# Norm seams of a two-block transformer kernel: feature sums, first product tiles and the place of the norm's scale

## The chip, the cores and the metric

One core of a Trainium2 chip runs the whole program. The metric is the device time of one execution in microseconds; the median of a few executions is compared. The engines are called PE (TensorE), DVE (VectorE), ACT (ScalarE), POOL (GpSimd) and SP (SyncE, which issues the weight loads).

## The reference

256 tokens with D = 1024 features go through a first block of two layers (beside a context of 256 tokens, which is needed until the last mixer) and a second block of two layers. Everything is float32. Cut to what matters:

```
# first block, layer l; x and the context xc alike
h  = x * (1 + scale1) + shift1
y  = mixers(h @ w_in)          # GLA, MLA, convolution module, gated and merged, @ w_out
x  = layer_norm(a * x + gate1 * y)                    # ln1
x  = layer_norm(a * x + gate2 * conv_ffn(x * (1 + scale2) + shift2))   # ln2
# inside the convolution module: silu(layer_norm(conv(h))) @ conv_wo

# second block, layer i
y  = attention(rms_norm(h, g_mix_pre[i]) @ w_in)      # stick-breaking, then dilated
h  = h + rms_norm(y @ w_out, g_mix_post[i])
f  = square(relu(rms_norm(h, g_ffn_pre[i]) @ w_ff_in[i])) @ w_ff_out[i]
h  = h + rms_norm(f, g_ffn_post[i])
h  = h + (p[i] @ w_ple[i]) * sigmoid(rms_norm(h, g_ple[i]) @ w_ple_gate[i])
```

Both norms run over the 1024 features of a token; the layer norm needs mean and mean square, the rms norm the mean square alone. At this point the context matters only in this: layer 0 works on 512 columns (256 tokens and 256 of context), layer 1 after its mixers and the second block on 256.

## The kernel before

The activations lie feature-major in SBUF: X is 8 feature tiles (KD = 8) of 128 partitions with a column for each token. So a norm's sum over features runs across partitions, and the kernel takes it on PE: `sums` (L904 to L910) multiplies each of the 8 feature tiles by a constant matrix of ones and adds the eight products in one PSUM tile, which then holds the sum in every partition. A layer norm needs two such tiles (`resid_sum`: X, and `resid_sq`: the squares that ACT makes), an rms norm one.

Weights come in 1 MB chunks into a ring of three (SP issues them, chunk n when chunk n-3 has been used). Every engine's program is written out by hand, block by block, and the class `Plan` (from L140) only fixes which PSUM bank (of 8) each tile gets, and the order of tiles and chunks; the engines' programs must follow that order.

Three forms of product stand at the seams.

- `cols` (L773): float32, one tile of 128 output features after another, for each tile 8 matmuls over k, the feature tile of the operand. The profile shows two records for each such matmul.
- `parts` (L743): layer 0's FFN `up` product. Operand and weights are split in a high half (fp32r) and a low half, and a tile takes three matmuls for each k. ACT makes the high half of the weights, POOL the low half (L726), two buffers of each.
- `narrow_cols` (L818, with `thrice` L811 to L816): the same three products in the second block, 256 columns. ACT makes the high half of a weight tile, `narrow_hi` (L1418), DVE the low half, `narrow_lo` (L2393); `narrow(u)` runs three tiles ahead of tile u, with four buffers.

A layer norm goes like this. ACT takes a product's tile out of PSUM with the gate as its scale (L1480), DVE adds it to X (`residual`, L2016), ACT squares X. When all tiles are done PE takes both sums. DVE forms mean and variance (`moments`, L1982 to L1992, from L1986), ACT the square root, DVE the reciprocal (L1973), then for each feature tile DVE subtracts the mean and multiplies (L2022, L2023), ACT applies gain and offset (`scaled`, L1488), and DVE modulates it by scale and shift (`operand_a`: L1941, or L1950 where the operand is split, with L1962 for the low half, and ACT the high half between). The first product tile runs through k as the operand arrives, and the second tile after it.

In the second block `post` (L2410) normalises a mixer's or the FFN's output and adds it to X (L2415, L2417); ACT squares X; PE sums; `rms` and `root` give 1/rms in the tile RS; `pre` (L2395) forms the operand X * g * RS on DVE (L2400), ACT rounds it to the high half, and DVE takes the low half (L2405). The FFN's relu is L2556 and its square L2558 with the split L2544; the gate of the last part (ple) is a sigmoid on ACT, with L2580 to L2582 on DVE.

The convolution runs on DVE. Its norm (`cln`) is summed on PE straight after the product cq, and DVE normalises right behind, before the two latent rms norms of MLA (L2295 to L2299). ACT's convolution sigmoids and DVE's products (L2305, L2306) come after the gate tiles co.0, and then ACT takes the tiles of the uq product (PE L1164) out of PSUM as mla_qn and mla_qr.

## Time and profile before

| | before |
|---|---|
| median of 3 runs | 3613.69 us (3610.08 to 3616.46) |
| profiled execution, its own time | 3616.7 us |
| its span | 3614.6 us |
| mean granted PE clock | .949 |
| PE busy | 3214.1 us, 89% of the span |
| DVE busy | 1715.0 us, 47% |
| ACT busy | 1024.0 us, 28% |
| POOL busy | 150.9 us, 4% |
| ACT_TABLE_LOAD at L1378 | 120 times |

How to read it: an engine's share is an average over stages with different limits, so PE's 89% doesn't say where the other 11% lie. The waits list for each engine what ended its idle time. A timeline row gives start and length in us (x16 means that sixteen instructions of a kind stand in it), and in brackets the idle time of the engine just before with what ended it. An operation whose line is that of a helper is told by its tile: L1378 is ACT's helper, so there the name behind it counts. The granted clock is a share of full speed, 1.00 for 2.4 GHz and .50 for 1.2 GHz.

### The profile page before, as it was taken

How to read it: one execution, taken by the hardware profiler on the slowest of the kernel's cores; microseconds unless marked ns; L12 is line 12 of the kernel's file. 1: busy time of each engine (PE TensorE's matmuls, PEld its weight loads, DVE VectorE, ACT ScalarE, POOL GpSimd, SP SyncE). 2: the span in 40 equal slices, each digit the busy share in tenths (PEclk: the TensorE clock that was granted, in tenths of full speed). 3: DMA queues.
4: the chain of work that ended last, by engine and by line, in shares of the span. 5: the costliest groups of instructions: out<-in, count | busy, mean ns of one | idle time of the engine just before them, and what ended most of it. 6: DMA issues, size and time to landing. Idle time of an engine off the chain costs nothing.

```text
span 3614.6 us, 38987 instructions
## 1 busy us (share of the span) xinstructions
PE 3214.1 (89%) x15931; PEld 2335.8 (65%) x15931; DVE 1715.0 (47%) x2857; ACT 1024.0 (28%) x1645; POOL 150.9 (4%) x125
## 2 busy tenths in 40 slices
PE   6978798999999789998988899989978898977898
PEld 3655454444444378743777666878877888975887
DVE  2268876241211268702367932235154655734555
ACT  3132210122230233202332033221145434423333
POOL 4000000000000044300000000000000000000000
PEclk9989799999999999998998999999999999978999
DMA  5221124322233222222221332334542454411552
GB/s 187 82 59 35 47 91 138 121 61 83 104 100 121 70 82 94 79 80 63 77 64 59 111 100 79 115 123 148 155 143 71 140 154 138 140 41 56 152 157 89
DMA packets 419440, 362.26 MB, mean 100 GB/s; under 512 B 20848, under 2 KB 392612, under 8 KB 419264
## 3 DMA queue, kind: packets, MB, share of 16 engines
q1 hardware_dynamic: 416928, 359.11, 31.6%
q8 instruction: 127, 2.08, 0.2%
q0 software_dynamic: 2336, 0.67, 0.1%
q14 instruction: 49, 0.40, 0.0%
HBM read 358.70 MB, written 1.05 MB: 100 GB/s over the span
## 4 chain that ended last, share of the span: by engine, by line
PE 73%; DVE 17%; issue 4%; ACT 4%; DMA 1%; POOL 1%; DVEq 0%; ACTq 0%; POOLq 0%
PE banks L783 13%; PE banks L893 13%; PE banks L758 7%; PE banks L875 6%; DVE conv_out L2145 5%; PE banks L814 4%; PE banks L815 4%; PE banks L816 4%; PE banks L805 3%; PE banks L909 3%; PE banks L1137 2%; ACT narrow_hi L1378 2%; PE banks L916 1%; PE banks L1128 1%; DVE gla_att L2207 1%
## 5 line engine op out<-in xcount | busy, mean ns | idle before, releaser
L2393 DVE TENSOR_TENSOR narrow_lo<-wring,narrow_hi 128x1024 fp32r<-128x1024 f32 x204 | 248.0, 1224 | 266.4 <-ACT narrow_hi L1378 265.8
L783 PE MATMUL banks<-operand_a,wring 128*128 128x256 f32 (+1 forms) x1184 | 345.4, 455 | 29.1 <-DVE operand_a L1941 29.1
L814 PE MATMUL banks<-operand_narrow,narrow_hi 128*128 128x256 f32 x960 | 289.4, 301 | 41.1 <-DVE operand_narrow L2405 24.3
L783 PEld LDWEIGHTS banks<-operand_a,wring 128*128 128x128 f32 x1184 | 228.8, 194 | 145.5 <-issue 121.3
L2145 DVE SCALAR_TENSOR_TENSOR conv_out<-conv_in,vectors,conv_out 128x512 f32<-128x512 f32 (+1 forms) x464 | 286.7, 618 | 15.2
L893 PE MATMUL banks<-operand_a,wring 128*128 128x512 f32 (+1 forms) x768 | 264.0, 499 | 22.7 <-DMA wring<-in_w_in_dram 13.6
L815 PE MATMUL banks<-operand_narrow,narrow_hi 128*128 128x256 f32 x960 | 276.4, 288 | 0.0
L816 PE MATMUL banks<-operand_narrow,narrow_lo 128*128 128x256 f32 x960 | 276.2, 288 | 0.0
L893 PEld LDWEIGHTS banks<-operand_a,wring 128*128 128x128 f32 x768 | 146.0, 194 | 132.9 <-issue 98.1
L1378 ACT ACTIVATE narrow_hi<-wring 128x1024 fp32r<-128x1024 f32 x204 | 212.0, 1049 | 67.6 <-PE banks L816 66.2
L875 PE MATMUL banks<-ffn_h,wring 128*128 128x512 f32 (+1 forms) x704 | 227.4, 486 | 0.0
L814 PEld LDWEIGHTS banks<-operand_narrow,narrow_hi 128*128 128x128 f32 x960 | 187.9, 196 | 55.6 <-issue 23.5
L1128 PE MATMUL banks<-operand_a,wring 128*128 128x512 f32 (+1 forms) x512 | 183.3, 515 | 19.3 <-DVE conv_in L2163 19.3
L875 PEld LDWEIGHTS banks<-ffn_h,wring 128*128 128x128 f32 x704 | 133.8, 190 | 92.9 <-issue 83.5
L815 PEld LDWEIGHTS banks<-operand_narrow,narrow_hi 128*128 128x128 f32 x960 | 189.4, 197 | 0.6
L893 PE MATMUL banks<-operand_b,wring 128*128 128x512 f32 (+1 forms) x512 | 174.5, 498 | 17.2 <-DMA wring<-in_mla_wo_dram 6.3
L816 PEld LDWEIGHTS banks<-operand_narrow,narrow_lo 128*128 128x128 f32 x960 | 189.0, 197 | 0.0
L726 POOL TENSOR_TENSOR weights_lo<-wring,weights_hi 128x1024 fp32r<-128x1024 f32 x44 | 108.9, 2476 | 1360.3 <-ACT weights_hi L1378 1360.3
L758 PE MATMUL banks<-operand_a_hi,weights_hi 128*128 128x512 f32 x352 | 138.0, 392 | 29.9 <-POOL weights_lo L726 29.9
L814 PE MATMUL banks<-ff_h,narrow_hi 128*128 128x256 f32 x512 | 149.1, 291 | 16.5 <-DVE ff_h L2544 11.2
L1128 PEld LDWEIGHTS banks<-operand_a,wring 128*128 128x128 f32 x512 | 102.6, 206 | 84.7 <-issue 76.8
L1378 ACT ACT_TABLE_LOAD x120 | 154.0, 1283 | 2.8 <-PEq L2603 0.7
(326 smaller groups left out, 5454.0 us busy)
## 6 DMA issues: line engine op xcount, KB each, us to landing
wring<-in_w_in_dram SPq DMA_DIRECT2D x52, 1024.0 KB, 5.1
wring<-in_w_ada_dram SPq DMA_DIRECT2D x48, 1024.0 KB, 6.4
wring<-in_ffn_wup_dram SPq DMA_DIRECT2D x44, 1024.0 KB, 5.0
wring<-in_w_ff_in_dram SPq DMA_DIRECT2D x32, 1024.0 KB, 5.4
wring<-in_w_ff_out_dram SPq DMA_DIRECT2D x32, 1024.0 KB, 5.7
wring<-in_ffn_wdown_dram SPq DMA_DIRECT2D x32, 704.0 KB, 4.6
wring<-in_w_in_dram SPq DMA_DIRECT2D x36, 512.0 KB, 5.0
wring<-in_w_in_dil_dram SPq DMA_DIRECT2D x18, 1024.0 KB, 4.9
```

Of the source, the lines that this page charges most:

```text
L726: pool.tensor_tensor(WL[:, u % 2, :, :], w, WH[:, u % 2, :, :].bitcast(F32), ALU.subtract).then_inc(ev("w_lo"), 1)
L758: mm = pe.matmul(bank(t, 0, n), w[:, k, :], x[:, k, 0:n], start=first, stop=last)
L783: mm = pe.matmul(bank(t, 0, n), w[:, k, j * P:(j + 1) * P], opnd[:, k, 0:n], start=k == 0, stop=k == kt - 1)
L814: pe.matmul(out, wh, a[:, 0:SEQ], start=first, stop=False)
L815: pe.matmul(out, wh, a[:, SEQ:512], start=False, stop=False)
L816: return pe.matmul(out, wl, a[:, 0:SEQ], start=False, stop=last)
L875: mm = pe.matmul(bank(t, 0, n), w[:, k % per, :], opnd[:, k, 0:n], start=k == 0, stop=k == kt - 1)
L893: mm = pe.matmul(bank(t + j, 0, n), w[:, k, j * P:(j + 1) * P], (AF if gate else opnd)[:, k, 0:n], start=k == 0, stop=k == KD - 1)
L1128: mm = pe.matmul(bank(t, 0, n), w[:, k, :], AF[:, k, 0:n], start=k == 0, stop=k == KD - 1)
L1378: act.activation(dst, src, f, **kw).then_inc(*inc)
L2145: own(stt(dst, src, w, dst, ALU.mult, ALU.add))
L2393: tt(NL[:, v % 4, :, :], w, NH[:, v % 4, :, :].bitcast(F32), ALU.subtract).then_inc(ev("narrow_lo"), 1)
```

## The change

It has five parts.

1. **Sums by DVE.** For ln1, ln2 and the convolution norm DVE keeps running totals over the eight feature tiles (X in `TD[0]`, the squares in `TD[1]`) while the product before still runs, seven adds each, and PE multiplies just the two totals by the ones.
2. **The layer norm's loop.** The first two centrings stand ahead of the wait for the square root. ACT does gain and offset and the modulation tile by tile, and the high half where there is one, DVE only the low half.
3. **First tiles together.** Of the next product the first tiles are taken together over k: the gate tile (in layer 1 with two key tiles), two tiles of `up` in layer 0 and four in layer 1, three tiles in the second block. For that, two weight splits move into the residual loop before, and the next weights are split one tile earlier (`more=4`); the first four low halves of the second block are POOL's.
4. **The second block's 1/rms at the exit from PSUM.** The operand is X * g alone. The squares' ones-matmuls stand between the product's matmuls. RS is applied by DVE at the eviction (Q and K of layer 0, relu, gate), through the cos and sin tables (layer 1), or as a scale for each token (V, for which PE turns RS in the tile `rc`). Bank 7 is kept for such small tiles.
5. **The convolution norm** moves behind co.0's gates and the latent norms.

The diff, cut to its core. On PE:

```diff
+        def moments(t, n, at=0):
+            for i in range(2):
+                start_tile(t + i)
+                counter("ln_sum", 1)(0)
+                pe.matmul(bank(t + i, 0, n), cn("ones"), TD[:, at + i, 0:n], start=True,
+                          stop=True).then_inc(*made(t + i))
...
-            cols_a(f"gr{l}", 512, a_ready())
+            first_tiles(512, a_ready(), (f"gr{l}", 1), *([(f"k{l}", 2)] if l else []))
...
             cols_a(f"cq{l}", n)
-            sums(F[f"cln{l}"], CV, 0, KD, n, lambda m: pe.wait_ge(ev("conv_out"), KD * l + m + 1))
-            sums(F[f"cln{l}"] + 1, SQC, 0, KD, n, lambda m: pe.wait_ge(ev("conv_sq"), KD * l + m + 1))
...
+            run(branch(f"co{l}", CV, n, None, (0,)))
             t = F[f"krr{l}"]
...
-            run(branch(f"co{l}", CV, n, None, (0,)))
+            moments(F[f"cln{l}"], n, 2)
...
-            for i, (name, src) in enumerate((("resid_sum", X), ("resid_sq", SQB))):
-                sums(F[f"ln1_{l}"] + i, src, 0, KD, n, counter(name, KD))
-            cols_a(f"up{l}", n, a_ready())
+            moments(F[f"ln1_{l}"], n)
+            first_tiles(n, a_ready(), (f"up{l}", 4 if l else 2))
+            cols_a(f"up{l}", n, 4 if l else 2)
...
+        def first_tiles(n, ready, *names):
+            for k in range(KD):
+                ready(k)
+                for t, pairs in tiles:
+                    for j, (w, x) in enumerate(pairs):
+                        mm = pe.matmul(bank(t, 0, n), w[:, k, :], x[:, k, 0:n], start=k + j == 0,
+                                       stop=k == KD - 1 and j == len(pairs) - 1)
+                    if k == KD - 1:
+                        mm.then_inc(*made(t))
...
+            for k in range(KD if ready else 0):
+                ready(k)
+                for i in range(together):
+                    mm = thrice(bank(t0 + i, 0, SEQ), v0 + i, k, AN[:, k, :], k == 0, k == KD - 1)
+                    if k == KD - 1:
+                        mm.then_inc(*made(t0 + i))
+                add(k - 1)
```

On ACT (DVE's `narrow` changes alike; the root that moves is the convolution norm's):

```diff
-        def narrow(u, more=3):
+        def narrow(u, more=4):
...
+        def high(g, m):
+            op(AN[:, m, 0:SEQ], X[:, m, 0:SEQ], ACT.Copy, (ev("n_hi"), 1), scale=vec(g, m))
+        def deviation2(x, t):
+            act.wait_ge(*done(t))
+            op(x, bank(t, 0, SEQ), ACT.Sqrt, free(t), scale=1.0 / D, bias=EPSC)
...
+        def operand_split(m):
+            modulated(TD[:, m % 2, :], 0, 3, m, 2).then_inc(ev("a_full"), 1)
+            act.wait_ge(ev("a_full"), m + 1)
+            op(AH[:, m, :], TD[:, m % 2, :], ACT.Copy, (ev("a_hi"), 1))
...
-            root(TD[:, 3, 0:n])
             for m in range(3, 5):
                 latent(m)
+            co = gates(f"co{l}", l, 2 * KD, n)
             root(TD[:, 0, 0:n])
             root(TD[:, 0, :])
-            co = gates(f"co{l}", l, 2 * KD, n)
             next(co)
             next(co)
+            root(TD[:, 3, 0:n])
```

On POOL, behind `down0`, and on DVE:

```diff
+        for v in range(4):
+            _, w = narrow_weights(v)
+            pool.wait_ge(ev("narrow_hi"), v + 1)
+            pool.tensor_tensor(NL[:, v, :, :], w, NH[:, v, :, :].bitcast(F32), ALU.subtract).then_inc(ev("narrow_lo"), 1)
...
+        def scale(t):
+            n_scale[0] += 1
+            dve.wait_ge(*freed(t))
+            dve.reciprocal(RS, RS).then_inc(ev("scale"), 1)
+            dve.wait_ge(ev("scale"), n_scale[0])
+
+        def post(t, name, g, g2):
+            dve.wait_ge(*freed(t))
+            own(dve.reciprocal(RSP, RSP))
+            for m in range(KD + 1):
+                if m < KD:
+                    dve.wait_ge(*freed(F[name] + m))
+                    own(stt(TD[:, m % 2, 0:SEQ], Y[:, m, :], vec(g, m), RSP, ALU.mult, ALU.mult))
+                    resid2[0] += 1
+                    tt(X[:, m, 0:SEQ], X[:, m, 0:SEQ], TD[:, m % 2, 0:SEQ], ALU.add).then_inc(ev("resid2"), 1)
+                    dve.wait_ge(ev("resid2"), resid2[0])
+                if m:
+                    operand2(g2, m - 1)
...
-                    ts(x, bank(t, 0, SEQ), 0.0, None, ALU.max).then_inc(*free(t))
+                    if m == 0 and h == 0:
+                        scale(F[f"fpre{l}"])
+                    stt(x, bank(t, 0, SEQ), 0.0, RS, ALU.max, ALU.mult).then_inc(*free(t))
```

How the instructions move, at three places. First ACT around layer 0's convolution norm (conv_sq are the squares of the convolution's output, the one tmp_dve row behind them the norm's square root, the two-fold one the latents' roots; tmp_act from banks are co.0's gates, tmp_act from conv_out the convolution's sigmoids). Before:

```order
L1378 ACTIVATE conv_sq<-conv_out 128x512 x8
L1378 ACT_TABLE_LOAD
L1378 ACTIVATE tmp_dve<-tmp_dve 128x512
L1660 ACTIVATE latents<-banks,vectors 128x512
L1378 ACTIVATE latent_squares<-banks,vectors 128x512
L1660 ACTIVATE latents<-banks,vectors 128x512
L1378 ACTIVATE latent_squares<-banks,vectors 128x512
L1378 ACTIVATE tmp_dve<-tmp_dve 128x512 x2
L1378 ACT_TABLE_LOAD
L1378 ACTIVATE tmp_act<-banks,vectors 128x512 x2
L1378 ACTIVATE tmp_act<-conv_out,vectors 128x512 x8
L1378 ACTIVATE mla_qn<-banks 128x512 x2
```

and with the change:

```order
L1473 ACT_TABLE_LOAD
L1473 ACTIVATE tmp_dve<-tmp_dve 128x512 x2
L1473 ACT_TABLE_LOAD
L1473 ACTIVATE tmp_act<-banks,vectors 128x512 x2
L1473 ACT_TABLE_LOAD
L1473 ACTIVATE tmp_dve<-tmp_dve 128x512
L1473 ACT_TABLE_LOAD
L1473 ACTIVATE tmp_act<-conv_out,vectors 128x512 x8
L1473 ACTIVATE mla_qn<-banks 128x512 x2
```

The norm's root went from ahead of the last two latents to behind the gates, with two more table loads.

Second, ACT from the last residual tile before the first FFN on. Before (operand_a_hi is the operand's high half, weights_hi the weights'):

```order
L1480 ACTIVATE tmp_act<-banks,mod 128x256 x2
L1378 ACTIVATE squares_b<-resid 128x512 x2
L1378 ACT_TABLE_LOAD
L1378 ACTIVATE tmp_dve<-tmp_dve 128x512
L1378 ACTIVATE resid<-resid,vectors 128x512 x8
L1378 ACTIVATE operand_a_hi<-tmp_dve 128x512 x8
L1378 ACTIVATE weights_hi<-wring 128x1024 x2
```

and with the change:

```order
L1473 ACTIVATE weights_hi<-wring 128x1024
L1607 ACTIVATE tmp_act<-banks,mod 128x256 x2
L1473 ACTIVATE squares_b<-resid 128x512 x2
L1473 ACT_TABLE_LOAD
L1473 ACTIVATE tmp_dve<-tmp_dve 128x512
L1473 ACTIVATE resid<-resid,vectors 128x512
L1558 ACTIVATE tmp_dve<-resid,mod 128x256 x2
L1473 ACTIVATE operand_a_hi<-tmp_dve 128x512
```

The weights' high halves stand ahead of the norm now, and scaling, modulation and high half follow one another for each feature tile.

Third, PE at the seam into the second block. Before:

```order
L875 MATMUL banks<-ffn_h,wring 128x256 x176
L909 MATMUL banks<-resid,consts 128x256 x8
L909 MATMUL banks<-squares_g,consts 128x256 x8
L909 MATMUL banks<-b_sq,consts 128x256 x8
L814 MATMUL banks<-operand_narrow,narrow_hi 128x256
L815 MATMUL banks<-operand_narrow,narrow_hi 128x256
L816 MATMUL banks<-operand_narrow,narrow_lo 128x256
```

and with the change, up to the second feature tile's square (L876):

```order
L864 MATMUL banks<-operand_narrow,narrow_lo 128x256
L862 MATMUL banks<-operand_narrow,narrow_hi 128x256
L863 MATMUL banks<-operand_narrow,narrow_hi 128x256
L864 MATMUL banks<-operand_narrow,narrow_lo 128x256
L876 MATMUL banks<-b_sq,consts 128x256
L862 MATMUL banks<-operand_narrow,narrow_hi 128x256
```

The 24 ones-matmuls ahead of the product are gone; two stand in their place (`L998 MATMUL banks<-tmp_dve,consts 128x256 x2`), and the rms norm's eight stand between the product's nine-fold steps.

## Rows read from the trace of the kernel before

**Rows 1.** The page: shares of the chain that ended last, and three groups by line

```profile
PE 73%; DVE 17%; issue 4%; ACT 4%; DMA 1%; POOL 1%; DVEq 0%; ACTq 0%; POOLq 0%
...
L2393 DVE TENSOR_TENSOR narrow_lo<-wring,narrow_hi 128x1024 fp32r<-128x1024 f32 x204 | 248.0, 1224 | 266.4 <-ACT narrow_hi L1378 265.8
...
L1378 ACT ACTIVATE narrow_hi<-wring 128x1024 fp32r<-128x1024 f32 x204 | 212.0, 1049 | 67.6 <-PE banks L816 66.2
...
L1378 ACT ACT_TABLE_LOAD x120 | 154.0, 1283 | 2.8 <-PEq L2603 0.7
```

**Rows 2.** Waits of PE: line, releaser: us in total, times, longest us

```profile
PE banks L909 <- ACT b_sq L1378: 35.4, 16, 13.5
...
PE banks L758 <- POOL weights_lo L726: 29.9, 1, 29.9
PE banks L783 <- DVE operand_a L1941: 29.1, 3, 16.8
```

**Rows 3.** Timeline, norm before the first FFN: start, us, engine, line, [idle before <- releaser]

```profile
1231.58 7.03 PE L909 MATMUL banks<-resid,consts 128*128 128x512 f32 x16
...
1232.65 0.69 DVE L2016 SCALAR_TENSOR_TENSOR resid<-resid,tmp_act 128x512 f32<-128x512 f32 x1 [6.17 <-ACT tmp_act L1480]
...
1247.43 3.35 DVE L1973 RECIPROCAL tmp_dve<-tmp_dve 128x512 f32<-128x512 f32 x1 [0.70 <-ACT tmp_dve L1378]
...
1252.27 0.81 ACT L1378 ACTIVATE resid<-resid,vectors 128x512 f32<-128x512 f32 x1 [4.87 <-DVE resid L2023]
...
1275.37 0.79 PE L758 MATMUL banks<-operand_a_hi,weights_hi 128*128 128x512 f32 x1 [29.90 <-POOL weights_lo L726]
```

**Rows 4.** Timeline of PE at the norm into layer 1 and layer 1's first norm

```profile
1668.13 7.03 PE L909 MATMUL banks<-resid,consts 128*128 128x512 f32 x16
...
1698.87 9.29 PE L783 MATMUL banks<-operand_a,wring 128*128 128x512 f32 x16 [16.85 <-DVE operand_a L1941]
...
2367.13 3.62 PE L909 MATMUL banks<-resid,consts 128*128 128x256 f32 x16
...
2384.62 8.62 PE L783 MATMUL banks<-operand_a,wring 128*128 128x256 f32 x28 [10.42 <-DVE operand_a L1941]
```

**Rows 5.** Windows: stretch, us, busy PE PEld DVE ACT POOL, granted clock, DMA share, GB/s

```profile
1699.00:1703.00 4.00, 4.00 (x5) 1.69 (x6) 4.00 (x14) 0.00 (x0) 0.00 (x0) 0.50 0.00 0
...
2649.00:2651.00 2.00, 1.56 (x10) 0.95 (x8) 1.68 (x5) 1.43 (x3) 0.00 (x0) 1.00 0.00 0
```

**Rows 6.** Timeline at the first uq tiles of layer 0

```profile
777.46 1.06 ACT L1378 ACTIVATE mla_qn<-banks 128x512 f32<-128x512 f32 x2
...
778.18 6.23 PE L1164 MATMUL banks<-operand_b,wring 128*128 128x512 f32 x10 [2.56 <-ACT mla_qn L1378]
```

**Rows 7.** Timeline of the second block's norms in layer 0

```profile
2614.96 3.62 PE L909 MATMUL banks<-resid,consts 128*128 128x256 f32 x16
...
2657.39 0.38 ACT L1378 ACTIVATE b_qk<-banks 128x256 f32<-128x256 f32 x1 [1.55 <-PE banks L816]
...
2783.48 3.62 PE L909 MATMUL banks<-b_sq,consts 128*128 128x256 f32 x16
...
2812.26 0.42 DVE L2556 TENSOR_SCALAR tmp_dve<-banks 128x256 f32<-128x256 f32 x1
...
3015.55 3.62 PE L909 MATMUL banks<-b_sq,consts 128*128 128x256 f32 x16
...
3023.21 0.42 ACT L1378 ACTIVATE b_sq<-resid 128x256 f32<-128x256 f32 x1 [2.80 <-DVE resid L2417]
...
3068.11 0.39 ACT L1378 ACTIVATE tmp_act<-banks 128x256 f32<-128x256 f32 x1 [1.54 <-PE banks L816]
```

**Rows 8.** Timeline of DVE and POOL in the first FFN

```profile
1304.85 0.75 DVE L2370 SCALAR_TENSOR_TENSOR tmp_dve<-ffn_up,vectors,tmp_dve 128x512 f32<-128x512 f32 x1
...
1306.73 2.40 POOL L726 TENSOR_TENSOR weights_lo<-wring,weights_hi 128x1024 fp32r<-128x1024 f32 x1 [3.04 <-ACT weights_hi L1378]
...
1306.88 2.79 DVE L2370 SCALAR_TENSOR_TENSOR tmp_dve<-ffn_up,vectors,tmp_dve 128x512 f32<-128x512 f32 x1
```

More of the change, by code:

```diff
@@ L175, in tiles, with gemm @@
             self.place(self.first[name] + j)
-    def gemm(self, name, chunks, split=lambda i: False, after=lambda: None):
-        self.reserve(name, sum(ends for _, ends in chunks))
-        self.chunk0[name], t = len(self.chunk_at), self.first[name]
+    def gemm(self, name, chunks, split=lambda i: False, after=lambda: None, done=0, total=0):
+        if not done:
+            self.reserve(name, total or sum(ends for _, ends in chunks))
+            self.chunk0[name] = len(self.chunk_at)
+        t = self.first[name] + done
         for i, (loads, ends) in enumerate(chunks):
@@ L831, in narrow_rows, with row_scale @@
+        def row_scale(l):
+            t = F[f"rc{l}"]
+            start_tile(t)
+            pe.wait_ge(ev("scale"), 3 * l + 1)
+            for tok in range(2):
+                mm = pe.matmul(bank(t, tok, tok + 1), RS[:, tok * P:(tok + 1) * P], cn("ident")[:, 0:1], start=True,
+                               stop=True)
+            mm.then_inc(*made(t))
         def narrow_rows(name):
@@ L1755, in _ @@
             ffn_sigmoid(FT1 - 1)
[L1756 to L1757 removed]
+            if l == 0:
+                residual(f"down{l}", l, 5, n, SQG, pl.last(f"wout{l}"))
+                scaled(l, "l2g", "l2b", n, operand(2, 1, 0, 2))
         resid2 = [0]
[L1761 to L1773 removed]
+        act.wait_ge(ev("eps_set"), 1)
@@ L2080, in _, with keys @@
                ALU.add).then_inc(*free(t))
+            def keys(m0, m1):
+                for m in range(m0, m1):
+                    t = F[f"k{l}"] + m
+                    dve.wait_ge(*done(t))
+                    ts(K[:, m, :], bank(t), vec(f"bk{l}", m), None, ALU.add).then_inc(*free(t))
+            keys(0, 2 * l)
             for m in range(8):
@@ L2105, in _ @@
             dve.wait_ge(*freed(F[f"z{l}"] + 7))
-            for m in range(4):
-                t = F[f"k{l}"] + m
-                dve.wait_ge(*done(t))
-                ts(K[:, m, :], bank(t), vec(f"bk{l}", m), None, ALU.add).then_inc(*free(t))
+            keys(2 * l, 4)
             for m in range(4):
@@ L2583, in _ @@
                 dve.wait_ge(ev("resid2"), resid2[0])
+            for m in range(KD):
+                t = F[f"pg{l}"] + m
+                narrow(pl.narrow_first[f"pg{l}"] + m)
+                dve.wait_ge(*done(t))
+                if m == 0:
+                    scale(F[f"ple{l}"])
+                tt(TA[:, m % 2, 0:SEQ], bank(t, 0, SEQ), RS, ALU.mult).then_inc(*free(t))
+                if m:
+                    add_row(m - 1)
+            add_row(KD - 1)
     core.close()
```

520 lines of the change are left out of this document (299 added, 221 removed).

## The prediction

> **What bounds the kernel now.** The time after an average over stages says little, so I read the views in this order. The page first: the chain that ended last is 73% TensorE (PE) and 17% VectorE (DVE) [rows 1]. So only two things can pay: PE work taken away, or PE waits closed. Next the waits of PE [rows 2]: three groups belong to norms, 35.4 us before ones-matmuls that wait for squares, 29.9 us before one L758 tile, and 29.1 us in three waits for a modulated operand. Then the timeline around each of those places [rows 3, 4, 6, 7], and the windows for the granted clock [rows 5]. In them the reader is to see that at each norm three costs stand behind one another: the feature sums on PE, a chain of small DVE and ScalarE (ACT) steps with PE idle, and a first product tile that must end before its evictor starts. The engines that take over the work, DVE and ACT, are idle there.
>
> I sum each seam from the last product before it to the point where the next steady stage is reached. Gains have a plus.
>
> **Layer norm before the first FFN (ln1, layer 0): +16.5.** Before, the first sums start at 1231.58 (7.03 us, and as much again for the squares), the reciprocal at 1247.43 (3.35 us), ACT's first scaling at 1252.27, and PE's first product at 1275.37, after 29.90 idle [rows 3]. A float32 matmul of 512 columns takes .86 (7.03 for eight); one of the three products takes a quarter, so a tile of 24 some 5.3, and two are done at 1288.8 with 2.8 for a slow start. After: the last totals end about 1235.5 (the residual row's successor: an eviction, one add into X and three adds at .7), two single matmuls .9, the variance, root and reciprocal chain (as in rows 3, 9.0 from the first sum's end less the 5.5 that DVE waited for the second, and 1.4 of centring hidden under the root), so the first normed tile stands at 1243.6. From there ACT feeds: scale .81 [rows 3], modulation in two halves, between 2 x .42 [rows 7] and 2 x .60, I take 1.0, high half .63, together 2.5 per feature tile: eight end at 1264. PE needs 1.4 per feature tile and follows: 1266. The next tile waits for its weight split, 1.05 [rows 1] on ACT and 2.40 on POOL [rows 8] behind an eviction: 1270 to 1272. That is 16.5 to 18.5 saved; I take the low end. If ACT's modulation took 1.2, 1.6 less.
>
> **Layer norm into layer 1 (ln2, layer 0): +16.5.** Before, sums at 1668.13, first product at 1698.87, and its 16 matmuls take 9.29 instead of 6.9 [rows 4], because PE's granted clock is .50 (1.2 of 2.4 GHz) for the first 4 us after the idle time [rows 5]. The 8 gate tiles follow, then the keys at 6.9 a tile. After: first operand 14 us after the sums' place, 1682, gate tile and two key tiles together, 6 matmuls of .43 per feature tile, 20.6, plus 2.2 for the low clock: 1704.9. Before, the same three tiles end at 1708.2 + 13.7. Saved 1721.9 - 1704.9 = 17; .5 off for the split key loop.
>
> **ln1, layer 1: +9.** Sums at 2367.13, product at 2384.62, four tiles until 2400.9 [rows 4]. After: first operand at 2375.9 (the reciprocal is 1.75 for 256 columns), four tiles of .43 make 1.73 per feature tile, 8 x 1.73 + 2.2 low clock: 2391.9.
>
> **Into the second block (ln2 of layer 1, first rms): +16.5.** Sums at 2614.96; PE idles 13.5 us before the squares' sums [rows 2]; the third tile's eviction is at 2657.39 [rows 7]. After: normed from 2622.2, three tiles together with one square matmul per feature tile, PE 1.51 (nine products at .12, a quarter of 3.62 / 8, and one square at .43), ACT 1.55 (scale, high, square). Four weight low halves now run on POOL, 2.40 each. The row at 1306.88 shows a DVE instruction of .75 becoming 2.79 while POOL's runs [rows 8]. That adds between 0 and 8 us; I take 3, because ACT and not DVE is the slowest feeder. Tiles at about 2640.
> By the Trainium skill, "GPSIMD Engine Reference", Key points, POOL shares its SBUF interfaces with VectorE, and DVE instructions with two SBUF inputs contend for them, which speaks against this part of the change. By that rule, with which the trace agrees, all four stand in the DVE chain, 4 x 2.0, and leave +11.5 here instead of +16.5.
>
> **The other rms seams.** Post and pre norm of layer 0's FFN: 2783.48 to the first relu at 2812.26 [rows 7]. After, six squares add 2.6 to the product, the sums (3.6) and the second norm's sums and root (about 8) leave, but the post loop gets a third DVE step (.42 to .48 for 128x256, as the ACT row at 3023.21 [rows 7], and some .05 between two): 1.48 x 8 from 2790.5, then PE's last column, root, reciprocal and four weight halves that are now taken one earlier: relu at 2809. **+3.2**. The one-earlier split also delays the second half's first relu by a high and a low half, 1.05 + 1.22 [rows 1], twice in all: **-4.3**. Layer 1's output product is half as long, too short for four weight splits ahead of it, so its seam gives nothing: **-.2**. FFN post norm and gate: 3015.55 to the last gate tile's eviction at 3068.11 [rows 7]; after, the product ends at 3018.1 with its squares, the root, the reciprocal and the pw evictions take 11.5, eight steps of 1.48 follow, three tiles are done at 3041.7, and five at 3.2 (high and low half, eviction) and the eviction follow: 3059.3, **+8.6**, and the same in layer 1, **+8.6**. Second mixer's pre norm: no norm chain ahead of 24 tiles, **+5**. Last add through one more DVE step: **-.5**. Scales of V rows, cos and sin tables and Q/K on DVE run beside PE: nothing, as ACT and DVE have idle time in those products; if that cover went, 16 x .42 = 6.7 us.
>
> **The convolution norm: -3.7 and -5.7.** This is the part where I go against the change. The sums leave PE (2 x 7.03, less two matmuls: 12 us), but PE is not what ends this stage: ACT evicts the uq tiles only after eight convolution sigmoids, and PE already waits 2.56 for that at 778.18 [rows 6]. The norm is now placed behind the gates and the latent norms, and ACT gets two more table loads per layer, 1.28 each [rows 1]. I place the last sigmoid at about 780, against 777 before, so the third tile starts 3 us later, PE idles some 17 us before, and .7 of low clock is added. Layer 1 is the same with no slack: 3.5 later and 2.2 of low clock. Bounds: if PE led, +12 and +5.2.
>
> Queues: SP's ring order is that of the plan, where only the keys' chunks stand around the gate tiles; each load is issued three chunks ahead, so nothing there is late.
>
> **The sum.** 16.5 + 16.5 + 9 + 16.5 + 3.2 - 4.3 - .2 + 8.6 + 8.6 + 5 - .5 - 3.7 - 5.7 = 69.5. The profiled execution took 3616.7; its span was 3614.6. 3616.7 - 69.5 = 3547.2. The median of the runs shown is 3.0 lower, so I forecast 3545 as the median.
>
> **Rivals.**
> - *PE led at the convolution norm* (.10). For: PE has 12 us less to do. Against: the 2.56 wait for ACT. +17 instead of -9.4: 3518.
> - *The fed phases stay slow for part of their time* (.13). PE is fed in drops, ACT-bound, and its clock had risen to 1.00 by 2649 in such a phase [rows 5]. If it falls again between drops, some 30 us are lost: 3575.
> - *The second block gives nothing* (.09). DVE's third step per tile, POOL against DVE, and earlier splits eat +3.2, +8.6 and +5: 3570.
> - *Slower: low clock throughout.* At full clock the matmuls of the phases taken together are 10.9 + 20.6 + 13.8 + 6 x 12.1 = 118 us. At .50 they take twice as long. From 70 us of these at half clock on, the gain is gone; all of it gives about 3650. For: the first 4 us at .50 after idle [rows 5]. Against: the window at 2649, 1.00 with PE busy 1.56 of 2.00 [rows 5]. (.03)
> - *The change doesn't do what it says* (.02). The totals on DVE could be on the path themselves: 14 adds of .7 per norm, if DVE were late in the product. DVE's wait of 6.17 for ACT before such a step speaks against it [rows 3]. Then each norm gives 5 less: 3570.
>
> **Chances.** My forecast .62; the two cases at 3570 and 3575 and the one at 3518 are taken in by the range: my own terms' bounds give 3530 to 3561, and the range is 3518 to 3577. A measurement of this kernel tells .2%, 7.2 us, from no change. Every case but the slow clock lies far below 3606; I give faster .95, same .01, slower .04, with some left for a wait that I don't see.
>
> **What would show it.** After: in the waits of PE no ones-matmul row above 5 us; L758's first wait near 11 us instead of 29.9; the modulated operand's longest near 9 instead of 16.8; each next product's first matmul starting while the norm's loop still runs on DVE; uq's third tile still waiting for ACT's mla_qn, about 3 us later after the convolution; four POOL rows near 2.4 just before the second block, with longer DVE rows beside them; clock .50 only in the first 4 to 5 us of each such phase. The prediction is wrong if the uq tiles start earlier with PE never waiting for mla_qn, if the clock stays at .50 through a whole fed phase, or if the three rms seams of a layer give under 5 us together.

## The result, and the profile after

The changed kernel takes 3583.44 us (median of 4 executions, 3580.98 to 3585.38) against 3615.07 for the kernel before: the ratio is .9912, with a 95% interval of .9895 to .9929, or 32 us faster. The forecast was 3545, the range began to be wrong above 3577, and of the forecast gain of 69.5 us less than half came. Its profiled execution has a span of 3581.4 us, 33.2 less than before.

The page of the changed kernel, the same lines as [rows 1]:

```profile
PE 70%; DVE 16%; ACT 6%; issue 6%; DMA 1%; POOL 1%; DVEq 0%; ACTq 0%; POOLq 0%
...
L1473 ACT ACTIVATE narrow_hi<-wring 128x1024 fp32r<-128x1024 f32 x204 | 213.0, 1051 | 161.6 <-PE banks L864 151.9
...
L1473 ACT ACT_TABLE_LOAD x124 | 159.1, 1283 | 2.9 <-PEq L2795 0.7
```

PE's busy time fell by 55 us (3214.1 to 3159.1), so PE did give up the work; but the span fell by 33 only, and its share of the last chain went from 73 to 70%, ACT's from 4 to 6. The waits of PE say what took its place, in the columns of [rows 2]:

```profile
PE banks L862 <- DVE operand_narrow L2561: 36.2, 7, 13.9
...
PE banks L1260 <- ACT mla_qn L1473: 29.8, 2, 17.6
PE banks L862 <- DVE tmp_dve L2736: 26.0, 34, 2.1
...
PE banks L862 <- DVE ff_h L2722: 23.1, 12, 3.2
...
PE banks L811 <- DVE operand_a_lo L2073: 14.4, 6, 10.2
PE banks L811 <- ACT operand_a L1558: 14.2, 2, 8.9
...
PE banks L876 <- ACT b_sq L1473: 8.7, 13, 2.7
```

The waits of [rows 2] are shorter (35.4 before ones-matmuls is 8.7, 29.9 is 10.2 for the longest, 29.1 is 14.2). In their place stand 29.8 us for ACT's mla_qn behind the convolution (4.5 before), which the prediction had foreseen, and 26.0 + 23.1 us for DVE in the FFN of the second block: L2736 is the relu, which frees PE's banks (no such wait before), and ff_h the operand of the second product (11.2 us before). That second pair it had not foreseen. The ones-matmuls still have two rows above the 5 us that the prediction allowed: the 8.7 here, and 9.1 at L998, four waits of at most 2.5.

To see where the time went, I took the same event in both traces at the end of each seam (before, after), and compared how far the changed kernel is ahead there.

| up to | before | after | gained here | forecast |
|---|---|---|---|---|
| convolution norm, layer 0: first mla_qn | 777.46 | 780.39 | -2.9 | -3.7 |
| ln1, layer 0: third FFN tile's eviction | 1294.22 | 1277.46 | 15.4, and 4.3 ahead of it | 16.5 |
| ln2, layer 0: keys and what follows | 2073.47 | 2041.15 | 15.6 | 16.5 |
| convolution norm, layer 1: fourth mla_qn | 2140.25 | 2113.62 | -5.7 | -5.7 |
| ln1, layer 1: second table load behind the first tiles | 2401.45 | 2365.80 | 9.0 | 9 |
| into the second block: last Q/K tile | 2694.83 | 2647.94 | 11.2 | 16.5 |
| FFN, layer 0: first relu | 2812.26 | 2763.25 | 2.1 | 3.2 |
| second half's first relu | 2916.14 | 2869.86 | -2.7 | -2.15 |
| post norm and gate: last gate tile | 3068.11 | 3033.84 | -12.0 | +8.6 |
| second mixer: last Q/K tile | 3159.88 | 3124.32 | 1.3 | 5 |
| FFN, layer 1: first relu | 3347.43 | 3313.31 | -1.4 | -.2 |
| second half's first relu | 3451.41 | 3419.69 | -2.4 | -2.15 |
| post norm and gate, layer 1 | 3606.91 | 3572.76 | 2.4 | 8.6 |

The 4.3 us in the second row lie between the convolution norm and the output product ahead of ln1, and no term of the forecast stands for them: 2.8 of them are PE's waits for three weight loads, which fell from 11.2 to 8.4. They are not the norm's: with the norm put back, the stretch from the first mla_qn to that product takes 396.0 us, in the changed kernel 394.8, before 399.1.

How far one execution can be trusted here can be read from the nine traces (this one, the control and seven of the experiments) whose program is the same up to this point. The first mla_qn comes anywhere from 777.7 to 784.7 in them, so the first row's -2.9 means little as a place. But counted from the first latent ahead of it, it comes after 79.04 or 79.05 us in all nine, against 76.05 before: 3.0 lost, and .9 more for the low clock behind PE's idle time. The seam of ln1 gives 15.2 to 17.3 us in the nine.

So the first five rows are right to about a microsecond each. What is missing is in the second block: 5 us at its entry, 20.6 and 6.2 at the two gates, 3.7 at the second mixer, 2 to 3 at the FFNs' starts. The three seams of a layer there (mixer or entry, FFN's start, gate) give 1.3 us together in layer 0 and 2.3 in layer 1; under 5 was the prediction's own sign of being wrong.

The first block's first norm, in the columns of [rows 3]:

```profile
1232.94 3.37 PE L998 MATMUL banks<-tmp_dve,consts 128*128 128x512 f32 x4 [2.54 <-DVE tmp_dve L2151]
...
1238.93 3.35 DVE L2081 RECIPROCAL tmp_dve<-tmp_dve 128x512 f32<-128x512 f32 x1
...
1243.05 0.81 ACT L1473 ACTIVATE resid<-resid,vectors 128x512 f32<-128x512 f32 x1 [4.81 <-DVE resid L2174]
...
1246.52 0.77 PE L811 MATMUL banks<-operand_a_hi,weights_hi 128*128 128x512 f32 x1 [10.21 <-DVE operand_a_lo L2073]
...
1253.92 0.50 PE L811 MATMUL banks<-operand_a_hi,weights_hi 128*128 128x512 f32 x1 [0.85 <-DVE operand_a_lo L2073]
```

The sums take PE 3 us instead of 14, the first product starts at 1246.5 instead of 1275.4, and then PE gets a feature tile every 2.5 us (each with about .85 idle): the forecast chain, step by step.

The clock is not as forecast everywhere. Two stretches of this seam and two at the entry to the second block, in the columns of [rows 5]:

```profile
1250.70:1267.60 16.90, 10.67 (x39) 6.53 (x38) 9.98 (x17) 14.73 (x24) 1.02 (x1) 1.00 0.00 1
1267.80:1274.40 6.60, 5.21 (x12) 4.13 (x13) 1.88 (x1) 0.14 (x1) 4.12 (x2) 0.50 0.18 52
2591.10:2598.80 7.70, 6.58 (x27) 6.11 (x28) 6.52 (x15) 7.54 (x17) 2.38 (x1) 0.50 0.72 246
2599.00:2607.00 8.00, 8.00 (x60) 7.70 (x59) 1.10 (x3) 1.97 (x5) 0.00 (x0) 1.00 0.01 2
```

Behind the phase that ACT feeds, in which PE was busy for 10.67 of 16.90 us, the granted clock fell to .50 once more, and at the second block's entry it stayed at .50 for the first 7.9 us of PE's work, not 4.

And the loop that holds the second block, DVE and then ACT in the first product of layer 0's FFN:

```profile
2780.72 1.23 DVE L2555 TENSOR_TENSOR narrow_lo<-wring,narrow_hi 128x1024 fp32r<-128x1024 f32 x1 [1.43 <-ACT narrow_hi L1473]
2781.86 0.42 DVE L2722 TENSOR_TENSOR ff_h<-tmp_dve,ff_h 128x256 fp32r<-128x256 f32 x1
2782.20 0.42 DVE L2736 SCALAR_TENSOR_TENSOR tmp_dve<-banks,gate_rank 128x256 f32<-128x256 f32 x1
2782.65 0.42 DVE L2738 TENSOR_TENSOR tmp_dve<-tmp_dve 128x256 f32<-128x256 f32 x1
2784.51 1.23 DVE L2555 TENSOR_TENSOR narrow_lo<-wring,narrow_hi 128x1024 fp32r<-128x1024 f32 x1 [1.43 <-ACT narrow_hi L1473]
```

```profile
2783.11 0.42 ACT L1473 ACTIVATE ff_h<-tmp_dve 128x256 fp32r<-128x256 f32 x1 [2.42 <-DVE tmp_dve L2738]
2783.43 1.04 ACT L1473 ACTIVATE narrow_hi<-wring 128x1024 fp32r<-128x1024 f32 x1
```

Read them as one chain: weight's low half, operand's low half, relu, square on DVE; copy and next high half on ACT; next low half on DVE. It closes every 3.79 us, while the 24 matmuls of a tile take 2.88, and neither engine is idle for a reason of its own. The relu period is 3.79 in both kernels, in all four half products. Two relus of the kernel before:

```profile
2819.84 0.42 DVE L2556 TENSOR_SCALAR tmp_dve<-banks 128x256 f32<-128x256 f32 x1
...
2823.62 0.42 DVE L2556 TENSOR_SCALAR tmp_dve<-banks 128x256 f32<-128x256 f32 x1
```

The gate's loop is another case. Before, ACT alone evicted its tiles and waited for PE (the 1.54 in the last row of [rows 7]), one tile every 2.88 us. In the changed kernel DVE scales the tile first, behind the weight's low half, and two of ACT's sigmoids stand 3.37 us apart:

```profile
3020.37 0.42 ACT L1473 ACTIVATE tmp_act<-tmp_act 128x256 f32<-128x256 f32 x1 [1.70 <-DVE tmp_act L2772]
...
3023.74 0.42 ACT L1473 ACTIVATE tmp_act<-tmp_act 128x256 f32<-128x256 f32 x1 [1.70 <-DVE tmp_act L2772]
```

This chain was made by the change. In layer 1, where no further weights have to be split, the last sigmoids stand 1.2 to 1.3 us apart.

### The profile page after: what moved, and what is told of

Same layout as the page of the kernel before. It is cut to its first block, busy times and chain, and to the rows that moved or that the text cites. A ratio compares the mean times of both kernels' runs of the same rounds, so it can differ in the third digit from the quotient of the medians.

```text
span 3581.4 us, 38780 instructions
## 1 busy us (share of the span) xinstructions
PE 3159.1 (88%) x15771; PEld 2306.4 (64%) x15771; DVE 1734.6 (48%) x2863; ACT 1049.8 (29%) x1685; POOL 160.7 (4%) x130
## 3 DMA queue, kind: packets, MB, share of 16 engines
HBM read 358.70 MB, written 1.05 MB: 100 GB/s over the span
## 4 chain that ended last, share of the span: by engine, by line
PE 70%; DVE 16%; ACT 6%; issue 6%; DMA 1%; POOL 1%; DVEq 0%; ACTq 0%; POOLq 0%
PE banks L982 13%; PE banks L830 12%; PE banks L779 6%; PE banks L964 6%; DVE conv_out L2306 4%; PE banks L853 3%; PE banks L862 3%; PE banks L864 3%; PE banks L863 3%; ACT narrow_hi L1473 3%; PE banks L1234 2%; PE banks L1013 2%; PE banks L1225 1%; PE banks L811 1%; DVE gla_att L2368 1%
## 5 line engine op out<-in xcount | busy, mean ns | idle before, releaser
L830 PE MATMUL banks<-operand_a,wring 128*128 128x256 f32 (+1 forms) x1056 | 298.8, 446 | 0.0
L2306 DVE SCALAR_TENSOR_TENSOR conv_out<-conv_in,vectors,conv_out 128x512 f32<-128x512 f32 (+1 forms) x464 | 286.8, 618 | 15.2
L830 PEld LDWEIGHTS banks<-operand_a,wring 128*128 128x128 f32 x1056 | 202.3, 192 | 97.2 <-issue 77.7
L982 PEld LDWEIGHTS banks<-operand_a,wring 128*128 128x128 f32 x768 | 147.2, 195 | 133.2 <-issue 98.7
L982 PE MATMUL banks<-operand_b,wring 128*128 128x512 f32 (+1 forms) x512 | 173.1, 495 | 15.2 <-DMA wring<-in_gla_wo_dram 6.7
L862 PE MATMUL banks<-ff_h,narrow_hi 128*128 128x256 f32 x512 | 152.9, 299 | 26.0 <-DVE ff_h L2722 23.1
L1225 PEld LDWEIGHTS banks<-operand_a,wring 128*128 128x128 f32 x512 | 101.4, 204 | 85.0 <-issue 77.5
L982 PEld LDWEIGHTS banks<-operand_b,wring 128*128 128x128 f32 x512 | 97.0, 193 | 82.0 <-issue 63.7
```

Of the source, the lines that this page charges most:

```text
L830: mm = pe.matmul(bank(t, 0, n), w[:, k, j * P:(j + 1) * P], opnd[:, k, 0:n], start=k == 0, stop=k == kt - 1)
L862: pe.matmul(out, wh, a[:, 0:SEQ], start=first, stop=False)
L982: mm = pe.matmul(bank(t + j, 0, n), w[:, k, j * P:(j + 1) * P], (AF if gate else opnd)[:, k, 0:n], start=k == 0, stop=k == KD - 1)
L1225: mm = pe.matmul(bank(t, 0, n), w[:, k, :], AF[:, k, 0:n], start=k == 0, stop=k == KD - 1)
L2306: own(stt(dst, src, w, dst, ALU.mult, ALU.add))
```

## The experiments

Each run is the changed kernel with one edit, unless it says otherwise; times are medians, ratios are to the kernel before on the same chip, with their 95% intervals.

**The changed kernel again.**

> The changed kernel once more, as the foot that the other runs are read against. Both theories: its ratio to before stays near .991, a time near 3583 us, and its trace shows the same stages as before: relu to relu 3.79 us in the FFN's first product, uq's third tile waiting some 17 us for ACT in layer 0.

Measured: 3580.32, ratio .9912 (.9897 to .9926). The medians of the changed kernel were 3583 and 3580, so below, differences of under 4 us are told only where a trace shows them. "Less" is against the control.

**The convolution norm put back.** Ones-matmuls, norm and root stand where they stood.

```diff
+            sums(F[f"cln{l}"], CV, 0, KD, n, lambda m: pe.wait_ge(ev("conv_out"), KD * l + m + 1))
+            sums(F[f"cln{l}"] + 1, SQC, 0, KD, n, lambda m: pe.wait_ge(ev("conv_sq"), KD * l + m + 1))
             cols_a(f"ckv{l}", 512)
...
-            moments(F[f"cln{l}"], n, 2)
```

> The convolution norm as it was before the change (ones-matmuls over all feature tiles behind cq, norm ahead of the latents), all else as changed. My theory, that this part of the change costs time: the sigmoids come earlier again, uq's third tile starts about 3 and 3 us sooner and the low clock behind PE's idle time goes, so 9 to 10 us less than the changed kernel, near 3574. Rival, that PE leads there and the sums were the cost: 12 us more for each layer, near 3600.

Measured: 3572.42, ratio .9891 (.9875 to .9908), 8 us less than the control. The intervals overlap, but the rival's 3600 is far off, and the trace has the two parts: from the first latent to the first mla_qn 75.6 us instead of 79.0, and in layer 1 from the sixth merged tile to the fourth mla_qn 67.3 instead of 72 to 74.

**The convolution norm between ckv and kr, totals on DVE kept.**

```diff
             cols_a(f"ckv{l}", 512)
+            moments(F[f"cln{l}"], n, 2)
             cols_a(f"kr{l}", 512)
...
             totals(3, SQC, n, lambda m: dve.wait_ge(ev("conv_sq"), KD * l + m + 1))
+            moments(F[f"cln{l}"], n)
...
```

The loop that normalises moves with it ahead of kr, and ACT's root ahead of the gates.

> The convolution norm's totals on DVE as changed, but the two ones-matmuls and the whole norm between the products ckv and kr instead of behind the gates. My theory, that the place and not the totals costs time: PE is 12 us earlier in layer 0 and 5 in layer 1, and the sigmoids, which need only the gates by then, follow: 20 to 26 us less than the changed kernel, near 3560. Rival, that PE now waits for DVE's totals behind the convolution: no better than with the norm put back, near 3574.

Measured: 3559.65, ratio .9851 (.9837 to .9866), 21 us less than the control. In its trace PE waits for no mla_qn at the place of [rows 6]; ACT reaches it 11 us earlier than in the changed kernel (780.39), and PE's 6.26 idle are for an operand of its own:

```profile
761.38 13.96 PE L1262 MATMUL banks<-operand_b,wring 128*128 128x512 f32 x25 [6.26 <-DVE operand_b L2463]
```

```profile
769.37 1.06 ACT L1475 ACTIVATE mla_qn<-banks 128x512 f32<-128x512 f32 x2
```

So the totals on DVE are worth 13 us (against the run with the norm put back), and the place behind the gates gave all of it back and another 8.

**Eviction ahead of the weight's low half, on DVE** (FFN, gate, and Q and K of layer 0).

```diff
                     x = TD[:, 2 + m % 2, 0:SEQ]
-                    narrow(pl.narrow_first[f"ffin{l}.{h}"] + m)
-                    if m:
-                        low_half(m - 1)
...
                     tt(x, x, x, ALU.mult).then_inc(ev("ff_full"), 1)
+                    if m:
+                        low_half(m - 1)
+                    narrow(pl.narrow_first[f"ffin{l}.{h}"] + m)
```

> On DVE alone, in the second block's products, the eviction of tile u (with the norm's scale and the square) stands ahead of the low half of weight tile u+4 instead of behind it. Theory A, that in these loops DVE and ACT form one chain (low half, eviction, square, ACT's copy, ACT's next high half, next low half: 3.79 us a tile in the FFN, 3.37 in the gate) and that this is where the expected gain was lost: the periods fall to PE's 2.9, that is 64 x .9 = 57 us, 16 x .45 = 7 us, and 1 to 2 us at each of five first tiles: 60 to 70 us less, near 3518. Theory B, that PE or the weight ring sets these periods: less than 10 us less, and the relu period stays above 3.5.

Measured: 3505.3, ratio .9701 (.9687 to .9716), 75 us less than the control, above the 60 to 70 expected. The chain is open, DVE now waits for PE:

```profile
2856.57 1.23 DVE L2555 TENSOR_TENSOR narrow_lo<-wring,narrow_hi 128x1024 fp32r<-128x1024 f32 x1
2858.29 0.42 DVE L2733 SCALAR_TENSOR_TENSOR tmp_dve<-banks,gate_rank 128x256 f32<-128x256 f32 x1 [0.50 <-PE banks L864]
2858.75 0.42 DVE L2735 TENSOR_TENSOR tmp_dve<-tmp_dve 128x256 f32<-128x256 f32 x1
2859.09 0.42 DVE L2722 TENSOR_TENSOR ff_h<-tmp_dve,ff_h 128x256 fp32r<-128x256 f32 x1
2859.45 1.23 DVE L2555 TENSOR_TENSOR narrow_lo<-wring,narrow_hi 128x1024 fp32r<-128x1024 f32 x1
```

2.88 from low half to low half, PE's own pace. Theory B is out.

**Squares two tiles behind.** In the FFN's last product PE's `add(m - 1)` becomes `add(m - 2)`, with the last two behind it.

> The changed kernel, but the ones-matmul of a square in the FFN's last product stands two tiles behind the tile it belongs to, not one. Theory A: PE waits there for ACT's square, some .5 us at each of seven tiles in both layers, so 6 to 8 us less, near 3574. Theory B, that these waits are idle time which the weights' arrival would give anyway: within 2 us of the changed kernel.

Measured: 3571.49, ratio .9879 (.9866 to .9893), 9 us less; the trace has 4.2 and 3.7 us in the two products. In the changed kernel each tile had a wait like this. With the lag they are gone (8.7 us in 13 waits became 2.7 in 2):

```profile
2957.99 0.70 PE L876 MATMUL banks<-b_sq,consts 128*128 128x256 f32 x2 [0.53 <-ACT b_sq L1473]
```

**One first tile alone in the second block.** `together` is 1 instead of 3.

> The changed kernel, but in the second block the first product tile alone is taken while the operand arrives, not three together. Theory A: in the FFN and the gate the loop of DVE and ACT sets the pace behind the first tile, so the two extra tiles that are ready early wait for their eviction and the seams of FFN and gate (four of six) lose nothing; the two seams before Q and K lose 3 to 5 us each: 5 to 10 us more, near 3590. Theory B, that PE's start was the gain: five to six us at each of six seams, 30 us more, near 3612.

Measured: 3569.84, ratio .9872 (.9859 to .9886): 10 us less, where both theories expected more. The three tiles taken together cost time. The windows of the changed kernel at the start of layer 0's FFN, in the columns of [rows 5]:

```profile
2744.50:2748.50 4.00, 3.94 (x18) 3.97 (x19) 3.79 (x10) 2.32 (x7) 0.00 (x0) 0.50 1.05 329
2749.00:2758.00 9.00, 9.00 (x67) 8.70 (x66) 3.97 (x9) 2.45 (x6) 0.00 (x0) 1.00 0.00 1
```

PE is saturated from its first matmul, at .50 for the first 4.5 us, and ends at 2758.8; DVE had fed the last feature tile by 2753.3. With one tile PE follows the feed, and the first relu comes at 2759.55 instead of 2763.25, with the product before it ending at the same time. And as the loop behind it takes 3.79 for each of 16 tiles, in order, two further tiles that lie ready in PSUM are worth nothing. The trace has 3.8 and 3.4 us at the two first relus, counted from the norm's first reciprocal, and 2 at each gate. At the entry the first Q tile comes 4.9 us earlier, and the last Q/K tile no earlier.

**The first low halves on DVE, behind the norm.** POOL's four instructions leave; DVE makes all four at the first Q tile.

> The changed kernel, but the second block's first four low halves are made by DVE as all others, not by POOL. Theory A, that POOL's 2.4 us instructions hold DVE's norm steps up (1.20 for .42, 1.80 for .42, 1.67 for .48 in the changed kernel's trace, and a wait): DVE's own 4 x 1.22 fall in the same stretch, three of them in its idle time before the norm, so 2 to 4 us less. Theory B, that POOL takes work off the path: 3 to 5 us more.

Measured: 3596.93, ratio .9943 (.9929 to .9956), 17 us more. The edit did more than it was meant to: it put the low halves behind the whole norm, and PE needs three before its first matmul:

```profile
2605.51 0.55 PE L858 MATMUL banks<-operand_narrow,narrow_hi 128*128 128x256 f32 x1 [19.73 <-DVE narrow_lo L2549]
```

**The same in DVE's idle time.** Two before the last residual tile, one before the moments, the last behind the norm.

> The changed kernel, with the second block's first low halves on DVE again, but in its idle time: two before the last residual tile, the third before the norm's moments, the fourth behind the norm. The first try had put all four behind the norm, and PE waited 19.73 us for them. Theory A, that POOL holds DVE up: DVE's steps fall back from 1.20, 1.80 and 1.67 to .42 and .48, the third half costs .8, PE waits for no low half: 2 to 3 us less. Theory B, that ACT feeds and DVE's delays don't count: within 1 us in the trace at the first Q tile.

Measured: 3575.27, ratio .9892 (.9878 to .9905). The ratio doesn't part it from the control; the trace does. First the changed kernel's DVE, then this one's:

```profile
2580.08 1.20 DVE L2147 SCALAR_TENSOR_TENSOR resid<-resid,tmp_act 128x256 f32<-128x256 f32 x1 [8.15 <-ACT tmp_act L1607]
...
2583.57 1.80 DVE L2096 TENSOR_TENSOR tmp_dve<-tmp_dve 128x256 f32<-128x256 f32 x1
```

```profile
2579.38 0.42 DVE L2152 SCALAR_TENSOR_TENSOR resid<-resid,tmp_act 128x256 f32<-128x256 f32 x1 [1.31 <-ACT tmp_act L1603]
...
2582.82 0.42 DVE L2092 TENSOR_TENSOR tmp_dve<-tmp_dve 128x256 f32<-128x256 f32 x1
```

From the last residual step to the first Q tile it takes 29.0 us (2579.38 to 2608.42) instead of 32.0 (2580.08 to 2612.06): the 3 us that the prediction had put down for POOL.

**Three tiles ahead.** `narrow(u, more=3)` on both engines.

> The changed kernel with the weights' halves made three tiles ahead as before, not four. Theory A: the first relu of each half no longer stands behind a high and a low half, 1.05 + 1.22 in the second halves (twice) and 1.2 to 2.3 at each first tile of six products: 8 to 12 us less, near 3571. Theory B, that the fourth tile then comes too late for PE: 1 to 2 us more at each of six products, near 3590.

Measured: 3562.1, ratio .9853 (.9839 to .9866), 18 us less, more than the 8 to 12 expected. By the trace 2 us come at each first relu, 3.3 at each second half (49.8 to 46.5 from the first half's last relu), and 4 in each FFN's last product, where ACT's copies and squares no longer stand behind a high half that waits for PE.

**The eviction order in the kernel before.** The same FFN edit there (without the gate).

> The kernel before, with one thing changed: in the FFN's first product of the second block DVE takes relu, square and the operand's low half ahead of the next weight's low half. Theory A, that the chain of DVE and ACT was in the kernel before already and the change only moved work in front of it: the relu period falls from 3.79 to 2.9, 64 x .9, near 3557, and nothing of it needs the change. Theory B, that the loop became slow by the change alone: within 5 us of the kernel before.

Measured: 3569.32, ratio .9871 (.9857 to .9884), 46 us less than the kernel before, 12 short of theory A, whose period of 2.88 its trace shows. The trace also shows what is missing: a half product of 16 tiles has 15 periods, and the four together give 53.6 us; 3.7 go between the halves of the FFNs and 3.7 between the last relu of layer 0 and the first of layer 1. So one reordering of DVE in the old kernel alone gives more than the whole change.

**The same edit in the changed kernel** (FFN only), to compare like with like.

> The changed kernel with the same single reordering as evict_before (relu, square and operand low half ahead of the weight's low half, in the FFN's first product only). Theory A, that part of the forecast gain was hidden behind the shared chain: the change is worth 50 to 65 us between this pair, so near 3512. Theory B, that the missing half is lost in the change's own parts and the chain cost both kernels the same: still 31 to 36 us between the pair, near 3535.

Measured: 3509.08, ratio .9704 (.9691 to .9717). Between this pair the change is worth 60 us, not 32: theory A. The difference of 28 is known to within about 9, an estimate from the three intervals. Tiles that lie ready now count, because DVE can take them at its own pace of 2.27:

```profile
2765.13 0.42 DVE L2733 SCALAR_TENSOR_TENSOR tmp_dve<-banks,gate_rank 128x256 f32<-128x256 f32 x1
...
2767.39 0.41 DVE L2733 SCALAR_TENSOR_TENSOR tmp_dve<-banks,gate_rank 128x256 f32<-128x256 f32 x1
```

Sixteen relus of a first half take 36.9 us here, 44.1 and 43.1 in the kernel before with the same edit, and 56.8 in both without it. From the first half's last relu to the second half's first it is 48.1 against 49.0; without the edit the change had lost 2.7 and 2.4 there. These two kinds of place give 20 of the 28 us.

**All together.** best3 has eviction order, convolution norm between ckv and kr, squares two behind, three tiles ahead; best1 the same with one first tile; best1_lo adds the low halves in DVE's idle time.

> The changed kernel with all that helped: eviction ahead of the weight's low half, norm of the convolution between ckv and kr, squares two tiles behind, three tiles ahead; three first tiles together. If the four gains are of separate stages: 75 for the eviction order, 21 for the convolution, 9 for the squares, and of the 18 of the lookahead only some 5, since the waits it took away are mostly those that the eviction order takes away too: near 3470. If they overlap further: 3480 to 3490.

> The same, but the first product tile of the second block alone. Theory A, that three tiles together lost only because the loop behind was a chain of DVE and ACT: now PE sets the pace behind, so the tiles taken together are PE work done early and one tile alone costs 1 to 2 us at each of six seams: 5 to 12 us more than with three. Theory B, that the loss lies in PE's own start (three tiles' work at the low clock before the first is done): 8 to 14 us less, as in the changed kernel.

> The fastest version so far (best1, 3473.5) with the first low halves on DVE in its idle time as in lo_dve2. Theory A, that POOL against DVE costs 3 us at the seam into the second block, in any version: near 3470. Theory B, that with one first tile alone PE needs the third half no longer at its start and nothing changes: within 1 us in the trace.

Measured: best3 3479.83 (.9620, .9607 to .9633), best1 3473.53 (.9606, .9592 to .9619), best1_lo 3468.72 (.9595, .9582 to .9608). The gains overlap by some 10 us more than the first sum. One tile against three: 6 us less, with intervals that overlap, but the traces agree: in best1 each FFN's first relu comes 3.6 and 3.4 us earlier, counted from the norm's first reciprocal, and the half behind it takes .9 longer (40.8 against 39.9). So with the loop open, too, three tiles together cost more than they bring. The low halves on DVE bring 1.35 us at the entry (25.01 to 23.66 from the last residual step to the first Q tile), neither the 3 of the one theory nor the less than 1 of the other; the medians can't tell more. The fastest version is 146 us faster than the kernel before, and 112 to 115 faster than the changed kernel.

## Why the prediction was wrong

**What held.** The method was right where PE or a plain feed sets the end: five seams of the first block within about a microsecond, the convolution norm's loss included (forecast -3.7 and -5.7, measured -3.0, -3.9 with the low clock behind it, and -5.7; the run with the norm put back is 8 us faster). So were the price of POOL against DVE at the entry (3), and nearly that of the deeper lookahead at the second halves (2.15 each, measured 2.7 and 2.4; a high and a low half, 1.05 + 1.22, would have been 2.27). Of the clock only the rough course held. The two rivals with 30 and 70 us of it did not come, but .50 lasted up to 7.9 us at the start of a fed phase and came back for 6.8 us behind the one in the first FFN (3.4 in the control, where the seam gives 1.8 us more). Over the whole span the granted clock was .945 against .949.

**Step one that failed: the end of a seam in the second block.** In "FFN post norm and gate" the sum took three tiles as done at 3041.7 and let "five at 3.2" follow. But done on PE isn't evicted. All eight evictions go through DVE's and ACT's loop, one behind the other, at up to 3.37 us, starting only behind root, high half, low half and reciprocal, 4.4 us after PE's last column. Measured from the first gate eviction (3010.94) to the last (3033.84) it is 22.9 us; 18.2 before. From PE's last column to the last eviction the sum had 17.6 us, and the trace has 27.8: 10.2 of the 20.6 missing at layer 0's gate. The 3.2 a tile stood for high half, low half and one eviction; scale on DVE and then sigmoid on ACT make two steps of it, and eight tiles go through them instead of five.

Another 3.8 are PE's: the trace shows it saturated where I had taken the feed as the pace, and the low clock of its first microseconds falls on the work of three tiles. The same is at the FFNs' starts, and at the entry, where the last feature tile was ready at 2601.2 and PE ended at 2607.7; the forecast's 2640, less the 35.65 us gained until there, is 2604.3. That the entry's 11.2 us come near the 11.5 that the prediction worked out for four full waits for POOL is chance, as POOL cost 3. The runs put 10 us on the three tiles (one_tile), and with the loop opened they don't pay either (best1 against best3).

**Step two: squares beside the product.** The sum had 2.6 us for six squares in a product. In the FFN's last product it is about 1.0 for each of eight tiles, because PE waits about .5 for ACT's square in order. lag2 measures 9 us for both layers together. Layer 0's last product ends 6.8 us later than the sum had it, and these are the rest (the three parts add up to 20.8, the forecast's own terms being rounded).

**Step three: one tile further ahead.** Priced at -4.3 at the halves; more3 measures 18. It also stands ahead of ACT's evictions in the last product (4 us in each), which the sum left out, and ahead of the reciprocal at every first tile, which it counted at the FFN's start alone. This and step two take in the same waits in the last product, so the two don't add up.

**The rival that should have been one of mine** was in the trace of before: a relu every 3.79 us against 2.88 of matmuls. I had seen that loop only as a stretch of the same length on both sides, and so as cancelling out. It doesn't: what was gained in front of this serial loop in form of tiles ready early was lost in it. The rival that "the second block gives nothing" named the right block, and of its three reasons one was right (the earlier splits, by more3); it had .09. About 28 us of what the change is worth are hidden by that chain (60 against 32 between the two pairs).

What stays open: where the 4.3 us ahead of ln1 come from, beyond the shorter waits for loads; the second mixer, whose seam gave 1.3 us instead of 5 and for which no run was made; where the last 8 of the 28 us lie; and how the three steps' sizes share what they have in common.

## What to carry to other kernels

Before pricing an earlier start, find what sets the period of the loop that follows: if its period is longer than the busy time of each engine in it (here 3.79 us against 2.88 of PE), it may be a chain through several engines' program orders, and work that was ready early was worth nothing in this one. In such a loop let each engine first do what frees another (evict, square), and what is only needed some tiles later (the next weights) behind it. Moving the convolution norm's sums off the matmul engine paid 13 us where the norm stayed in its place; moved behind other work it cost 21, more than the sums did.

## What the runs showed of the hardware

A DVE instruction with two operands in SBUF grew from .42 to 1.20 or 1.80 us, and one of .48 to 1.67, when POOL ran a 128x1024 subtraction of 2.4 us, as [rows 8] had shown at 512 columns. One that read PSUM (L2094, at 2583.11) kept its .42 in the same time. "GPSIMD Engine Reference", Key points, of the Trainium skill states that POOL shares its SBUF interfaces with VectorE and that DVE instructions with two SBUF inputs contend for them, and the trace agrees. But the price at the seam was 3 us, not the 8 of adding up four such waits: only these three instructions grew, by 3.4 us together, and the first of POOL's met an idle DVE.

PE started each fed phase at a granted clock of .50, also where it was then saturated. It had 1.00 after 4.1 us in the first FFN, 4.5 in the second block's first FFN and 7.9 at that block's entry, and in the first FFN it fell to .50 once more for 6.8 us, in a product behind a phase with PE busy for 10.67 of 16.90 us.
